# Query and up tiles of the selection stage as plain float32, candidate sums on GpSimd, heads interleaved

## The reference

```python
q = (xt @ w_query).reshape(T, PEER_HEADS, 2, HALF_Q)
scores = jnp.einsum('thpc,hpnc->thpn', q, sub_keys)
top_s, top_i = lax.top_k(scores, PEER_TOPK)               # 16 of 128 keys, both halves of 8 heads
cand_s = top_s[:, :, 0, :, None] + top_s[:, :, 1, None, :] # 16 x 16 sums
best_s, best_pos = lax.top_k(cand_s, PEER_TOPK)           # 16 of them
gate = jax.nn.softmax(best_s, axis=-1)
act = gelu(einsum('cd,ced->ce', xc, expert_u[ic]))
y = einsum('ce,ced->cd', gate * act, expert_v[ic])
```

## Time and profile before

| | |
|---|---|
| median of three runs | 3029.4 us |
| the profiled execution | 3030.18 us, its span 3028.4 us |
| PE busy | 97% of the span |
| DVE, ACT, POOL busy | 63%, 45%, 5% |
| granted TensorE clock, mean | 0.992 |
| stage of the change | about 160 to 357 us in the first layer, 1156 to 1354 us in the second |

### The profile page before, as it was taken

How to read it: one execution, slowest core, us unless ns; L and a number is a source line. 1 busy time by engine, 2 the same in 40 slices (tenths; PEclk the granted TensorE clock), 3 DMA queues, 4 the chain that set the end, 5 groups by cost and what they waited for, 6 DMA issues and landing times. The chain is left out here.

```text
span 3028.4 us, 53515 instructions
## 1 busy us (share of the span) xinstructions
PE 2933.2 (97%) x20746; PEld 2583.7 (85%) x20746; DVE 1912.8 (63%) x3655; ACT 1350.6 (45%) x2061; POOL 147.2 (5%) x76
## 2 busy tenths in 40 slices
PE   8998999999999999999999999999998999999898
PEld 7688889899898877888989989889876988887797
DVE  4489864788646647997468874674635466553556
ACT  4442344444444544334444444445524444552444
POOL 0052000000000004400000000010000001000000
PEclk9999999999999999999999999999999999999999
DMA  5243355544545524335554455554334454324454
GB/s 204 98 173 136 124 194 180 194 154 152 192 183 187 188 98 167 140 110 191 186 185 163 151 183 188 199 193 154 112 139 153 181 194 181 140 98 162 158 184 149
DMA packets 68021, 493.57 MB, mean 163 GB/s; under 512 B 7576, under 2 KB 7584, under 8 KB 8352
## 3 DMA queue, kind: packets, MB, share of 16 engines
q1 hardware_dynamic: 67568, 490.42, 45.0%
q0 software_dynamic: 304, 1.06, 0.1%
HBM read 490.39 MB, written 1.06 MB: 162 GB/s over the span
## 5 line engine op out<-in xcount | busy, mean ns | idle before, releaser
L788 DVE TENSOR_TENSOR ring_l<-ring,tile_h 128x1024 fp32r<-128x1024 f32 x648 | 764.8, 1222 | 670.8 <-ACT tile_h L743 666.6
L743 ACT ACTIVATE tile_h<-ring 128x1024 fp32r<-128x1024 f32 x644 | 645.7, 1051 | 531.5 <-PE ps L674 445.3
L642 PE MATMUL ps<-x_h,tile_h 128*128 128x256 f32 x2016 | 575.5, 285 | 1.2 <-issue 1.2
L643 PE MATMUL ps<-x_l,tile_h 128*128 128x256 f32 x2016 | 570.0, 283 | 0.0
L644 PE MATMUL ps<-x_h,ring_l 128*128 128x256 f32 x2016 | 569.9, 283 | 0.0
L642 PEld LDWEIGHTS ps<-x_h,tile_h 128*128 128x128 f32 x2016 | 386.4, 192 | 1.9 <-issue 1.5
L643 PEld LDWEIGHTS ps<-x_l,tile_h 128*128 128x128 f32 x2016 | 386.5, 192 | 0.2
L644 PEld LDWEIGHTS ps<-x_h,ring_l 128*128 128x128 f32 x2016 | 386.3, 192 | 0.0
L747 ACT ACTIVATE arena<-ps 128x512 f32 (+1 forms) x160 | 95.6, 597 | 436.1 <-PE ps L644 345.4
L672 PE MATMUL ps<-tile_h,w_even 128*128 128x512 f32 x640 | 249.5, 390 | 3.6 <-DVE w_even L813 3.6
L672 PE MATMUL ps<-tile_h,w_odd 128*128 128x512 f32 x640 | 249.3, 390 | 0.6 <-DVE w_odd L813 0.6
(11 more groups left out here) (328 smaller groups left out, 5542.8 us busy)
## 6 DMA issues: line engine op xcount, KB each, us to landing
ring<-stream SPq DMA_DIRECT2D x464, 1024.0 KB, 4.8
cs<-consts SPq DMA_DIRECT2D x1, 1712.5 KB, 8.5
x<-x_in SPq DMA_DIRECT2D x1, 1024.0 KB, 4.9
arena<-scratch POOLq DMA_DIRECT2D x1, 1024.0 KB, 7.7
out<-x SPq DMA_DIRECT2D x2, 512.0 KB, 2.7
tab<-table SPq DMA_DIRECT2D x1, 1.0 KB, 8.3
scratch<-arena POOLq DMA_DIRECT2D x1, 12.0 KB, 5.9
```

The source lines that it names most:

```text
L642: nc.tensor.matmul(out, uh[:, c, f], x_h[:, c, :], start=(c == 0), stop=False)
L643: nc.tensor.matmul(out, uh[:, c, f], x_l[:, c, :], start=False, stop=False)
L743: nc.scalar.activation(tile_h[:, j % 2, n], slot(k + j)[:, n], ACT.Copy).then_inc(hi_ready, 1)
L788: nc.vector.tensor_tensor(low_of(k + j)[:, n], slot(k + j)[:, n], tile_h[:, j % 2, n].bitcast(F32), ALU.subtract).then_inc(lo_ready, 1)
```

## The change

It touches the selection stage of both layers.

1. Query tiles 2 to 7 and up tiles 0 to 6 are plain: 13 tiles a layer. ACT's high parts and GpSimd's low parts of them are gone.
2. The candidate sums are made by GpSimd (`pool_sums`), two instructions for a head, for both token tiles at once; DVE waits for `cand_ready`.
3. DVE does the key steps of head h in turn with the sum steps of head h - 2.
4. Each reduction over 16 one-hot products is now a fold of four additions (8, 4, 2, 1 wide).
5. Five up tiles lie ahead of the gates: four, the transposes of token tile 0, the fifth, the transposes of token tile 1. The 32 gate groups stand among the 11 other up tiles; DVE makes the last pieces of `selT` for one token tile, then its 16 groups, then the same for the other.

```diff
--- before.py
+++ after.py
-EARLY = 10
+EARLY = 5
...
-        cand = room(TT * PAIRED).rearrange("p (t n) -> p t n", t=TT)
+        cand = room(2 * TT * PAIRED).rearrange("p (b t n) -> p b t n", b=2, t=TT)
...
-        FIRST_WQ = 2
-        SPLIT_UPS = 7
-        AHEAD = 8 - FIRST_WQ + SPLIT_UPS
...
-        def pe_early(pe, l, n, bank):
...
-        def act_early_high(act, l, n):
...
-        def pool_early_lows(pool, l):
-            for n in range(AHEAD):
...
+        def pool_sums(pool, l):
+            for h in range(8):
+                pool.wait_ge(top_ready, l * 8 + (h + 1))
+                one, two, c = top[:, :, 2 * h, :], top[:, :, 2 * h + 1, :], cand[:, h % 2, :, :]
+                nc.gpsimd.tensor_tensor(c[:, :, 0:16 * WIDE].rearrange("p t (a b) -> p t a b", a=WIDE),
+                                        one[:, :, 0:WIDE].unsqueeze(3).to_broadcast([P, TT, WIDE, 16]),
+                                        two.unsqueeze(2).to_broadcast([P, TT, WIDE, 16]), ALU.add)
+                nc.gpsimd.tensor_tensor(c[:, :, 16 * WIDE:PAIRED].rearrange("p t (a b) -> p t a b", b=NARROW),
+                                        one[:, :, WIDE:16].unsqueeze(3).to_broadcast([P, TT, 16 - WIDE, NARROW]),
+                                        two[:, :, 0:NARROW].unsqueeze(2).to_broadcast([P, TT, 16 - WIDE, NARROW]),
+                                        ALU.add).then_inc(cand_ready, 1)
...
-            return min(GROUPS, (4 * at + 10) // 11)
+            return min(GROUPS, (2 * at + 5) // 11)
...
             for h in range(8):
-                if h == FIRST_WQ:
-                    pe.wait_ge(xl_ready, 2 * l + 2)
                 if h >= 2:
                     pe.wait_ge(wq_ev, l * 8 + (h - 1))
-                if h >= FIRST_WQ:
-                    pe_early(pe, l, h - FIRST_WQ, 4 + h % 2)
-                else:
-                    arrived(pe, 1, l, A_WQ + h)
-                    up = up_features(chunks(A_WQ + h), xT, 4 + h % 2) if h else \
-                        up_as_turned(pe, 2 * l + 1, chunks(A_WQ), 4, norm_and_keys_read)
-                    up.then_inc(tile_done, 1)
+                arrived(pe, 1, l, A_WQ + h)
+                up = up_features(chunks(A_WQ + h), xT, 4 + h % 2) if h else \
+                    up_as_turned(pe, 2 * l + 1, chunks(A_WQ), 4, norm_and_keys_read)
+                up.then_inc(tile_done, 1)
...
             def early_up(j):
                 pe.wait_ge(u_act, g + (j + 1))
-                if j < SPLIT_UPS:
-                    pe_early(pe, l, 8 - FIRST_WQ + j, 4 + j % 2)
-                else:
-                    arrived(pe, 1, l, A_EXP + j)
-                    up_features(chunks(A_EXP + j), xT, 4 + j % 2).then_inc(tile_done, 1)
+                arrived(pe, 1, l, A_EXP + j)
+                up_features(chunks(A_EXP + j), xT, 4 + j % 2).then_inc(tile_done, 1)
 
             pe.wait_ge(wq_ev, l * 8 + 8)
-            for j in range(EARLY - 1):
-                early_up(j)
-            pe.wait_ge(key_ev, l * 8 + 8)
-            for tt in range(TT):
+            def turn_chosen(tt):
                 pe.wait_ge(chosen_ready, l * TT + (tt + 1))
                 for c in range(3):
                     last = nc.tensor.transpose(ps[tt][:, c * P:(c + 1) * P], chosen[:, tt, c, :], ident)
                 last.then_inc(sel_mm, 1)
+
+            for j in range(EARLY - 1):
+                early_up(j)
+            pe.wait_ge(key_ev, l * 8 + 8)
+            turn_chosen(0)
             early_up(EARLY - 1)
+            turn_chosen(1)
...
                 queries_out(h)
-                act_early_high(act, l, h)
                 if h < 3:
                     scores_out(h)
...
-                if 8 + j < AHEAD:
-                    act_early_high(act, l, 8 + j)
                 act_apply(act, 1, l, A_EXP, j // 4, j % 4, ACT.Gelu)
-                if j == 5:
+                if j == EARLY - 2:
                     for tt in range(TT):
                         act.wait_ge(g_diff, l * TT + (tt + 1))
                         nc.scalar.activation(gexp[:, tt, :, :], gexp[:, tt, :, :], ACT.Exp).then_inc(g_exp, 1)
...
+            chosen_out(0)
             act_apply(act, 1, l, A_EXP, (EARLY - 1) // 4, (EARLY - 1) % 4, ACT.Gelu)
+            chosen_out(1)
...
-                for tt in range(TT):
-                    nc.vector.scalar_tensor_tensor(cand[:, tt, 0:16 * WIDE].rearrange("p (a b) -> p a b", a=WIDE),
-                                                   one[:, tt, 0:WIDE].unsqueeze(2).to_broadcast([P, WIDE, 16]), 0.0,
-                                                   two[:, tt, :].unsqueeze(1).to_broadcast([P, WIDE, 16]), ALU.add, ALU.add)
-                    last = nc.vector.scalar_tensor_tensor(
-                        cand[:, tt, 16 * WIDE:PAIRED].rearrange("p (a b) -> p a b", b=NARROW),
-                        one[:, tt, WIDE:16].unsqueeze(2).to_broadcast([P, 16 - WIDE, NARROW]), 0.0,
-                        two[:, tt, 0:NARROW].unsqueeze(1).to_broadcast([P, 16 - WIDE, NARROW]), ALU.add, ALU.add)
-                step.after(last)
...
+            def side_by_side(*heads):
+                for _ in zip(*heads):
+                    pass
+
+            for h in range(2):
+                side_by_side(key_steps(h))
+            for h in range(2, 8):
+                side_by_side(key_steps(h), sum_steps(h - 2))
+            side_by_side(sum_steps(6), sum_steps(7))
...
-                    step.after(nc.vector.tensor_reduce(chosen[:, tt, s, :], hot, AX.X, ALU.add))
+                    for w in (8, 4, 2):
+                        step.after(nc.vector.tensor_tensor(hot[:, :, 0:w], hot[:, :, 0:w], hot[:, :, w:2 * w], ALU.add))
+                    step.after(nc.vector.tensor_tensor(chosen[:, tt, s, :], hot[:, :, 0], hot[:, :, 1], ALU.add))
...
-            carry_wait()
-            base = l * (2 * GROUPS)
-            with dve.Fori(0, GROUPS // 2) as i:
-                for b in range(2):
-                    one_hot(0, base, 2 * i, 16 * i + 8 * b, b)
+                carry_wait()
+                with dve.Fori(tt * GROUPS // 4, (tt + 1) * GROUPS // 4) as i:
+                    for b in range(2):
+                        one_hot(0, base, 2 * i, 16 * i + 8 * b, b)
...
-                pool_early_lows(pool, l)
+                pool_sums(pool, l)
```

More of the change, by code:

```diff
@@ L1312, in dve_block1, with key_steps @@
             dve_split_x(dve, 2 * l + 1)
-            for h in range(8):
+            def key_steps(h):
+                rows = [(tt, 2 * h + s) for tt in range(TT) for s in range(2)]
                 dve.wait_ge(key_ev, l * 8 + (h + 1))
-                rows = [(tt, 2 * h + s) for tt in range(TT) for s in range(2)]
                 carry_wait()
@@ L1320, in dve_block1 @@
                     last = nc.vector.max(top[:, tt, r, 0:8], sc[:, tt, r, :])
-                step.after(last)
+                done = step.mark(last)
+                yield
+                step.until(done)
                 carry_wait()
@@ L1344, in dve_block1, with sum_steps @@
-                step.after(last)
+                    last = nc.vector.max_index(topi[:, tt, r, 8:16], top[:, tt, r, 8:16], sc2[:, n, :])
+                yield
+            def sum_steps(h):
+                c, c2 = cand[:, h % 2, :, :], cand2[:, h % 2, :, :]
+                dve.wait_ge(cand_ready, l * 8 + (h + 1))
                 carry_wait()
                 for tt in range(TT):
-                    last = nc.vector.max(best[:, tt, h, 0:8], cand[:, tt, :])
-                step.after(last)
+                    last = nc.vector.max(best[:, tt, h, 0:8], c[:, tt, :])
+                done = step.mark(last)
+                yield
+                step.until(done)
@@ L1354, in dve_block1 @@
+                done = step.mark(last)
+                yield
+                step.until(done)
                 carry_wait()
                 for tt in range(TT):
-                    last = nc.vector.max(best[:, tt, h, 8:16], cand2[:, tt, :])
-                step.after(last)
+                    last = nc.vector.max(best[:, tt, h, 8:16], c2[:, tt, :])
+                done = step.mark(last)
+                yield
+                step.until(done)
                 carry_wait()
                 for tt in range(TT):
-                    last = nc.vector.max_index(pos[:, tt, h, 8:16], best[:, tt, h, 8:16], cand2[:, tt, :])
+                    last = nc.vector.max_index(pos[:, tt, h, 8:16], best[:, tt, h, 8:16], c2[:, tt, :])
```

44 lines of the change are left out of this document (16 added, 28 removed).

## The result

| | before | after |
|---|---|---|
| median, side by side on one chip | 3029.5 us (3028.5 to 3030.3, 4 runs) | 3070.2 us (3069.5 to 3071.4, 4 runs) |
| ratio | | 1.0133, 95% interval 1.0119 to 1.0147 |
| profiled execution, span | 3030.2, 3028.4 us | 3070.3, 3068.0 us |
| first query tile to first down tile, first layer | 159.93 to 356.84 = 196.9 us | 156.48 to 375.58 = 219.1 us |
| the same, second layer | 1156.05 to 1353.30 = 197.3 us | 1174.91 to 1393.11 = 218.2 us |

A forecast was written before the change was run, and what follows sets the result against it. PE, busy 97% of the span, was taken as the bound. Matmuls 14.8, transposes 0.6 and waits 13.4 less 9.6 gave 19.1 us, second layer 19.5; 38.6 on 3030.2 made about 3068 us, range 3055 to 3078.

The forecast's parts named there:

- What is added to PE: Query and up tiles: a plain tile costs 1.14 us more than a split one, 14.8 us a layer for thirteen.
- DVE's stalls go: Candidate sums: DVE's stalls beside GpSimd's low parts, 16.4 us in the first layer, vanish.
- When DVE is done: Selection: rounds of 7.69 us, heads bound by PE; selection ends at 245.5, token tiles ready at 258.3 and 270.2 us.
- The fold: One-hot products: four additions take 1.8 us instead of a 2.29 us reduction, 0.5 saved; other end 2.4 us.
- The four waits: PE waits 5.5 and 4.2 us for token tiles 0 and 1, 1.7 at the first gate group, 2.0 at the down tiles.
- The clock: Slow PE rows behind the new waits: 0 to 1.1 us a layer, taken as 0.
- before's 9.6: PE time to be won per layer at most: 8.0 us wait, 0.5 at the down tiles, 1.1 slow tile.
- ACT's Exp in time: Gate values: Exp stands behind the fourth up tile, 252.8 us, is wanted at 257.4, and is in time.
- GpSimd's sums: Candidate sums on GpSimd: 0.5 us for both, or 4.8 at full duration; up to 3.2 us a layer, taken as none.
- The waits vanish: Rival: DVE gains more and all four PE waits go, 5.8 us a layer, 3041 us; chance 0.08 for 3036 to 3055.
- The tail is late: Rival: slow folds, late sums and one slow clock piece add 6.7 us a layer, 3082 us; chance 0.09 above 3078.
- Not slower: Rival: the plain tile costs less than read, under 0.7 us extra with no wait left; chance 0.03.

The follow-up runs named there:

- Experiment 1: The kernel before with only query tiles 2 to 7 and up tiles 0 to 6 made plain: 3039.3 us, ratio 1.0035.
- Experiment 4: The changed kernel with PE's waits filled by 8, 6 and 4 matmuls whose results nobody reads: 3067.1 us, ratio 1.0129.
- Experiments 2: The changed kernel with ten up tiles ahead of the gates, gate groups in before's places, Exp behind the ninth up tile: 3069.5 us, ratio 1.0136.
- 6: The changed kernel with the heads in turn, a head's sums right behind its keys, nothing interleaved: 3070.0 us, ratio 1.0137.
- experiment 7: The changed kernel with the heads in turn and ACT's Exp behind the third up tile instead of the fourth: 3064.3 us, ratio 1.0117.
- experiment 3: The changed kernel with ten up tiles ahead of the gates and ACT's Exp behind the fourth up tile: 3043.0 us, ratio 1.0043.
- experiment 10: As experiment 9, but GpSimd makes the sums of heads 3 to 7 behind later low parts: 3012.4 us, ratio 0.9945.
- experiment 9: The changed kernel with before's 13 split tiles, ten early up tiles, Exp behind the fourth, GpSimd's sums between low parts: 3024.6 us, ratio 0.9989.
- experiment 11: As experiment 10, but with ten split up tiles, 16 split tiles a layer: 3037.2 us, ratio 1.0025.
- experiment 12: As experiment 10, but with eight split up tiles, 14 split tiles a layer: 3015.1 us, ratio 0.9952.
- experiment 5: The changed kernel with one reduction over 16 in place of each fold of four additions: 3069.1 us, ratio 1.0132.

## Why the prediction was right

The forecast of 3068 us missed by 2.2, and both its direction and its mechanism hold. Point by point:

- *What is added to PE.* Right: 14.8 us a layer. A plain tile in the trace of after is 6.91 us (two from 184.50 to 198.32). Experiment 1 has the price beside the vanished wait, 10.8 measured and 11.6 forecast for that kernel.
- *DVE's stalls go.* Right: no operation of the selection is above 0.3 us (up to its end at 241.94), and DVE then waits for PE's key scores, 21.7 us in seven times; 4.8 of them stand ahead of head 0, where before had 5.0. The 16.4 us were worth little because the heads come no faster than PE makes them, as the prediction said.
- *When DVE is done.* A round took 7.07 us (185.34 to 192.41) and not 7.69: the alternation did save the waits that the prediction left out. Counted from the start of the up tiles the selection ended at 18.4 us instead of 20.35.
- *The fold.* 2.04 us, 0.29 saved and not 0.5, as the third addition took 0.39 us and the last 0.39. The Trainium skill (VectorE: DVE Perf Modes, What auto-detection actually checks) gives the double rate to an operation whose tensors are all 16-bit with step one; the trace agrees for the first, 1024 columns in 0.69 us, as in the earlier trace rows, where 1024 columns of float32 (L399) took 1.18.
- *The four waits.* Forecast 5.5, 4.2, 1.7, 2.0, together 13.4; measured 3.99, 3.05, 1.98, 1.86, together 10.9. The first is shorter by the rounds (2.0) less 0.5 of a longer tail. The second is shorter because the slow fifth tile, 1.6 us, has eaten into it, less 0.4 by which DVE was longer from the first positions to the second (12.26 us, forecast 11.9).
- *The clock: a term that was mis-sized.* The prediction took 0, on the ground that another wait swallows a slow piece. That held for the fifth up tile. Behind the third wait no wait follows: the group and the twelve matmuls there lost 0.6 + 1.9 = 2.5 us in the first layer, 0.6 + 1.6 = 2.2 in the second, above the 1.1 of the upper bound. Experiment 4 shows the clock as the cause. The waits and their slow pieces are 10.9 + 1.6 + 2.5 = 15.0 us, against 13.4 forecast: with 14.8 + 0.6 and less before's 9.6 that is 20.8, where 20.5 was measured. The short waits (2.5 less) and the slow rows (4.1 more) were errors of opposite sign. That the total came out within 2.2 us of the forecast is luck; that it lies in the range is not.
- *ACT's Exp in time.* True by 0.5 us. The prediction had 4.6 us between the end of the fourth up tile and DVE's asking for it and gave no figure for what is left; it was 3.0 us, as DVE asked 1.5 us earlier behind the up tiles' start, and Gelu, table load and Exp take 2.5 of them. Experiments 2, 6 and 7 show it as the next bound.
- *GpSimd's sums.* 0.75 us a head where 0.5 was taken for the two and 4.8 was the other end; nobody waited for them.
- *The rivals.* "The waits vanish" was right as a price, 3041 us: experiment 3, which makes them vanish, measured 3043.0. What it takes is not a faster DVE but more up tiles ahead. "The tail is late" did not come: the folds were 2.04 us and the sums hidden. "Not slower" asked for a plain tile that costs under 0.7 us more, and it costs 1.14.

What stays open: what the interleave is worth with the Exp in an earlier place, which was not tried (with the interleave DVE doesn't wait for the Exp, so there may be nothing to gain, and experiment 7 with the heads in turn is 5.9 us faster than after); which part of the new selection brings experiment 10 its 17.1 us; why the program's start differs by up to 3.5 us between executions, and its first query tile by 1.7; and why some waits of 2 to 3 us are followed by slow rows and others not.

## What to carry to other kernels

A slower form of work on the bound engine must be paid by waits that exist: count them first, here 9.6 us against 14.8. When a consumer's work is moved earlier, list everything that its producer still waits for, down to a line on a third engine and to the step behind the one in question: one Exp behind the wrong tile was worth 26 us here, and a one-hot group 5. The new selection paid in experiment 10, which keeps the fast tiles and the ten up tiles ahead, has the Exp early, and puts GpSimd's short sums behind low parts by whose end their data is there. That last point alone was worth 12 to 13 us (experiments 9 and 10).

## What the runs showed of the hardware

- While GpSimd subtracts without a gap (1024 columns, 2.4 us each), DVE's operations with two inputs took 2.1 to 2.2 us more each, whatever their own length. The Trainium skill (SBUF — State Buffer, SBUF: two separate sides) has the pair of ports as an exclusive lock that a DVE operation with two inputs in SBUF and a GpSimd operation hold in turn, for a whole instruction; the trace of experiment 11 agrees, with 3.32 us against 1.23. One operation with a single input was held up as well: in experiment 10 the CAST at the start of the tail (256 columns, uint32 to bf16) took 4.86 us beside GpSimd and 0.28 without. The MAX8 and FIND_INDEX8 operations were not. GpSimd's own short additions of 128 and 96 columns (0.40 and 0.35 us) held up nothing, but they ran beside the selection's one-input operations only.
- Behind PE's waits of 2 to 4 us in after the next rows lost 1.1 to 2.5 us, in the two stretches of 20 us of the profile that were granted 0.83 and 0.91 of the full clock. With the wait filled by useless matmuls the next tile kept its usual 7.07 us, in a stretch granted 1.00. A wait of that length is not enough by itself: behind the 2.55 us of experiment 12, which stand alone, no row was slow and the granted clock stayed at 1.00. A slow piece costs nothing where a wait on another engine follows it: without it that wait was longer by about as much (experiment 7). How long the piece behind the last wait is differs too: from the start of the gate group to the next one it was 5.9 us in after and 4.8 in experiment 5, where 3.4 is usual.
